# Output projection: one group of twelve matmuls moved ahead of a wait, eighteen others moved back

## What is computed

```python
h = rmsnorm(x, g_mix)
u, q, k, v = split(h @ w_in)                     # w_in: 1024 x 2048
mixed = concat(pool(u), dilated_attention(q, k, v))
x = x + mixed @ w_out                            # w_out: 1024 x 1024
h2 = rmsnorm(x, g_ffn)
logits = h2 @ w_router + b_router                # top 4 of 32 experts
for e in range(32):
    gu = h2 @ w_gu[e] + b_gu[e]                  # 1024 x 2048
    x += combine[:, e] * (swiglu(gu) @ w_down[e] + b_down[e])
out = rmsnorm(x, g_final)
```

## Time and profile before

| | |
|---|---|
| time, median of 3 runs | 1019.98 us (1018.63 to 1020.21) |
| span of the profiled execution | 1018.5 us (its own time is not listed beside it) |
| TensorE matmul busy | 961.3 us (94%) |
| VectorE / ScalarE / GpSimd busy | 285.9 / 133.6 / 15.1 us |
| DMA traffic | 419.63 MB, mean 412 GB/s over the span |

### The profile page before, as it was taken

The page is one execution under the profiler, slowest core; times in us unless marked ns, Lnnn a source line. Parts: engine busy times, 40 slices in busy tenths (PEclk is TensorE's granted clock), DMA queues, the critical chain, the costliest instruction groups (busy, mean ns, idle before and its releaser), DMA issues.

```text
span 1018.5 us, 11652 instructions
## 1 busy us (share of the span) xinstructions
PE 961.3 (94%) x4851; PEld 423.1 (42%) x4851; DVE 285.9 (28%) x537; ACT 133.6 (13%) x200; POOL 15.1 (1%) x17
## 2 busy tenths in 40 slices
PE   8999999999998998989899898989899898999996
PEld 8988443434342342424243242424334342434332
DVE  5963531322222113112122212212211311222123
ACT  6634200000101000000001000000100000010002
POOL 0500000000000000000000000000000000000000
PEclk9999999999999899989999999999989998999998
DMA  9678999999999999999999999999999999999994
GB/s 353 220 329 365 411 426 420 431 426 431 430 434 432 428 429 430 423 430 435 427 432 432 429 431 427 430 436 434 431 429 426 429 432 431 433 427 432 425 425 200
DMA packets 26903, 419.63 MB, mean 412 GB/s; under 512 B 4228, under 2 KB 4888, under 8 KB 8920
## 3 DMA queue, kind: packets, MB, share of 16 engines
q1 hardware_dynamic: 26832, 419.15, 97.0%
q10 hardware_dynamic: 40, 0.01, 0.0%
HBM read 418.11 MB, written 1.05 MB: 412 GB/s over the span
## 4 chain that ended last, share of the span: by engine, by line
PE 55%; DMA 40%; DVE 3%; ACT 1%; issue 0%; SPq 0%; DVEq 0%
PE ps L1008 53%; DMA raw<-in_w_gu 37%; DMA raw<-in_w_down 3%; DVE woutl L736 1%; PE ps L1277 1%; PE ps L1332 1%; ACT sm L552 0%; PE ps L1019 0%; PE ps L1118 0%; DVE biased L931 0%; DVE mxs L753 0%; DVE sm L748 0%; DMA cst<-in_consts 0%; PE ps L1172 0%; DVE acc L987 0%
## 5 line engine op out<-in xcount | busy, mean ns | idle before, releaser
L1008 PE MATMUL ps<-raw,xT 128*64 128x512 f32 x2032 | 471.3, 614 | 44.4 <-DMA raw<-in_w_gu 44.0
L1008 PEld LDWEIGHTS ps<-raw,xT 128*64 128x64 f32 x2032 | 142.9, 141 | 344.2 <-issue 283.5
L1008 PE MATMUL ps<-raw,actT 128*64 128x512 f32 x1024 | 232.3, 595 | 0.9 <-DMA raw<-in_w_down 0.7
L1008 PEld LDWEIGHTS ps<-raw,actT 128*64 128x64 f32 x1024 | 70.5, 137 | 134.8 <-issue 129.4
L931 DVE TENSOR_TENSOR biased<-ps,biasT 128x1024 f32<-128x1024 f32 x32 | 39.2, 1225 | 294.7 <-PE ps L1277 294.7
L618 ACT ACTIVATE gu<-ps 128x1024 f32<-128x1024 f32 x32 | 32.8, 1025 | 526.1 <-PE ps L1008 526.1
L948 DVE TENSOR_TENSOR acc<-ps,acc 128x512 f32<-128x512 f32 x60 | 38.9, 687 | 175.8 <-PE ps L1008 175.8
L832 DVE TENSOR_TENSOR xT<-ps,gT 128x512 f32<-128x512 f32 x32 | 22.1, 692 | 166.0 <-PE ps L1008 165.8
L1008 PE MATMUL ps<-ysc,dispT 64*128 64x512 f32 x256 | 65.5, 613 | 0.0
L1008 PEld LDWEIGHTS ps<-disp,h 128*128 128x128 f32 x512 | 58.4, 192 | 12.4 <-issue 12.2
L1008 PE MATMUL ps<-disp,h 128*128 128x128 f32 x512 | 61.7, 278 | 0.2 <-DVE disp L826 0.2
(11 more groups left out here) (162 smaller groups left out, 445.6 us busy)
## 6 DMA issues: line engine op xcount, KB each, us to landing
raw<-in_w_gu SPq DMA_DIRECT2D x55, 4096.0 KB, 33.4
raw<-in_w_down SPq DMA_DIRECT2D x62, 2048.0 KB, 31.4
raw<-in_w_gu SPq DMA_DIRECT2D x16, 2048.0 KB, 12.3
win<-in_w_in SPq DMA_DIRECT2D x16, 512.0 KB, 14.0
wout<-in_w_out SPq DMA_DIRECT2D x4, 1024.0 KB, 9.4
raw<-in_w_down SPq DMA_DIRECT2D x4, 1024.0 KB, 36.1
early<-in_w_gu SPq DMA_DIRECT2D x1, 2048.0 KB, 11.5
raw<-in_w_gu SPq DMA_DIRECT2D x2, 1024.0 KB, 8.4
```

The source lines that it names most:

```text
L1008: return pe.matmul(out_, lhsT, rhs, start=start, stop=stop, skip_group_check=shared)
```

## The change

Only TensorE's written order changes; no instruction is added, removed or altered, and SyncE's, ScalarE's and VectorE's streams are the same.

```diff
             project(1, 0, range(4))
+            project(1, 1, range(4)).then_inc(half_projected, 1)
             pe.wait_ge(ymix_dve, 1)
             project(0, 0, range(4, DC))
             project(0, 1, range(4, DC)).then_inc(projected, 1)
-            project(1, 1, range(4)).then_inc(half_projected, 1)
...
+            project(1, 0, range(4, 6))
             pe.wait_ge(added, 1)
             turn_chunks(0, range(4), 4).then_inc(h2_turned, 1)
             turn_chunks(0, range(4, DC), 5).then_inc(h2_turned, 1)
-            project(1, 0, range(4, 6))
+            project(1, 0, range(6, DC)).then_inc(projected, 1)
             pe.wait_ge(wrt_scaled, 1)
             pe.wait_ge(h2T_act, 1)
             pe.wait_ge(h2T_dve, 1)
             route(0, range(DC)).then_inc(logits, 1)
-            project(1, 0, range(6, DC)).then_inc(projected, 1)
             project(1, 1, range(4, 6))
             pe.wait_ge(half_added, 1)
```

## The result

The changed kernel takes 1021.55 us (median of 21 runs, 1020.38 to 1022.99) against 1019.98 us (median of 21 as well): 1.57 us more, a ratio of 1.0016 with an interval of 1.001 to 1.0022. That is inside the 0.2% taken for no change and inside the range of 1018.0 to 1022.0; but it is a real small loss, where the forecast had +0.2 us. The profiled execution took 1021.75 us with a span of 1019.9 us.

What follows compares the result with a forecast made beforehand. The stream of weights on the DMA queues was taken to bound most of the run. Terms: -4.13 us old hole, +4.03 new hole, +0.3 down projection, net +0.2: median 1019.98 to 1020.2 us, range 1018.0 to 1022.0.

Steps and rivals of the forecast that it cites:

- The earlier issue: SyncE, after `half_projected`: issues at 83.05 us, 5.45 us earlier, so two loads land in line and 4.13 us are won.
- the hole at 86 us: Weight stream at 86 to 89 us, 11 GB/s: costs 4.13 us, all of which the change was to gain there.
- TensorE's chain: From tile 0's projection to the first expert: router at 92.02, tile 1's transposes at 96.12, all behind 1.00 us late.
- the wait on line 793: TensorE before tile 1's transposes: a new wait of 0.94 us for VectorE's add, which stands behind its top-k.
- The clock rival: TensorE's clock falls to half in the new wait: 2.76 us lost, end at 1023.0 us; chance 0.07.
- The hole that closes and does not open again: Rival for the stream from 86 us: loads come 4.13 us earlier for good, 1015.9 us; chance 0.04.
- The price of a lone load: Slot 7, into an idle queue: 2048 KB takes 8.6 us, landing at 106.74 against 106.84; 7.2 us as other end.
- The fit of 2.0 us and the bytes at 436 GB/s: Alternative for a lone 2048 KB load: an estimated 6.8 us, slack 2.6 us, sum -1.6 us; set aside for 8.6.
- a load's slack: Loads behind slot 7: time to landing less 8.6 us alone; tightest found 0.8 us, later ones have more.
- the down projection: Load issued at 128.76: 0.8 us of slack, now issued 1.00 us later, lands 0.2 us late; term +0.3 us.
- sign of being wrong: Slot 7 issued before 95 us, clock under 1.00 behind the wait, or another stream pause between 107 and 324 us.
- The rival without the wait: TensorE before tile 1's transposes: late by 0, not 1.00 us; -0.8 to -2.2 us, 1017.8 to 1019.2; chance 0.15.

Runs made afterwards that it cites:

- add_first: On the changed kernel, VectorE's add of tile 1's first half moved ahead of its top-k of tile 0; 1020.7 us, ratio 1.0009.
- late_supply: On the changed kernel, load into `early` issued right behind slot 7's and later slots freed sooner, VectorE's order kept; 1020.16 us, ratio 1.0003.
- late_only: On the kernel before, five more 128x512 matmuls on an unused bank ahead of TensorE's wait for half_added; 1022.03 us, ratio 1.0022.

## Why the prediction was right, and where it was off

The earlier issue was right: the two loads went out at 82.99 and 83.36 (said: 83.05), landed about 4 us sooner, and the hole at 86 us closed.

TensorE's chain was right to a tenth: tile 0's router at 92.05 (said 92.02), tile 1's transposes at 96.12 (said 96.12), all behind them 1.05 us late (said 1.00), the wait on line 793 in VectorE's written order. The clock rival is refuted: the granted clock stayed at 1.00. The hole that closes and does not open again is refuted by the row at 97 to 99 us.

The price of a lone load was off. I took 8.6 us for slot 7 and kept 7.2 as the other end; it took 7.2, and 7.2 to 7.4 in every experiment that moved the hole. The fit of 2.0 us and the bytes at 436 GB/s in the Trainium skill, "DMA: Bandwidth & Descriptors", section "Anatomy of one DMA — SWDGE (gpsimd) path", gave an estimated 6.8, nearer than the row that I preferred, though these loads are issued by SyncE. In the four kernels that leave the hole at its place its load took 8.4 to 8.7 us; why more there, no run shows. By itself this made the changed kernel better than forecast at that point: -1.4 us, not -0.1.

The step that failed is the sentence that a load's slack is its time to landing less 8.6 us, with +0.3 us for the one load that runs out of it, the down projection. There it held: 5.1 us behind the load in front instead of 4.9. By that rule `early`, with 11.5 us, had 2.9 us to spare and I did not look at it again. Measured, issued 1.05 us later and with slot 7 in sooner, it landed 8.4 us after its predecessor instead of 5.7. That term, 2.7 us, was missing; with slot 7's -1.4 it gives the +1.3 us at `early` and at the down projection, and the median's +1.6 us is of that size. No sign of being wrong that I named caught it, since the stream did not pause but flowed more slowly. That the time still fell inside the range was in part luck: the two errors had opposite signs, and with 7.2 us for a lone load the sum would have said -1.2 us. A load that comes into a queue that is running out cost more here than the time for which the queue would have stood empty.

The rival without the wait is answered by add_first: its -0.8 to -2.2 us did not come, +0.8 did. So TensorE's wait is not the whole cause, nor is the slow `early`: taking away either left a loss. Both taken away together, with the later slots freed sooner, made the kernel faster than before. late_supply, which keeps the wait and has little loss, speaks for the thin queue as the larger part; late_only, which loses without a moved hole, speaks against it. How the 1.6 us divide between TensorE's lateness and the thin queue is not settled, since each cure exposes the next thin load, a late slot is itself what makes the queue thin, and late_only lost more in its usual executions than its one profile shows.

## What to carry to other kernels

When a transfer is issued sooner, ask which transfer behind it finds the queue empty then; a hole in a stream is closed only if every load behind it can move as well. Read for each load how much of the stream still lies ahead of it at its issue, and treat a few microseconds (here, less than about 4) as already thin. Filling one engine's wait by matmuls that covered another moves the wait; it showed here in the written order of a third engine, where a reordered add removed it.

## What was not expected of the hardware

Loads issued late into a draining queue did not leave the DMA engines idle: they showed a share of 0.98 to 1.01 and moved 311 GB/s (135 to 137 us in add_first) or 367 GB/s (104 to 111 us in the changed kernel) against some 430 in a full queue. With 3.3 to 3.6 us ahead, nine of the ten loads of 2048 KB between slot 7 and the down projection landed 6.0 to 8.5 us after their predecessor (the tenth, in late_supply, 5.0), with 3.8 to 4.7 us ahead such loads landed 4.9 to 5.9 us after it, with 4.8 us or more 4.8 to 6.0. Why they move more slowly then, no run here shows, nor what makes the single steps of up to 1.7 us in a full queue.
